# Seven block products for four up groups of a feed-forward layer, between plain groups

## The reference

```python
        h = rmsnorm(x, ffn_norm[l])
        u = causal_dwconv(h @ w_up[l], conv_w[l], conv_b[l])
        a, b = jnp.split(u, 2, axis=-1)
        x = x + (jax.nn.silu(a) * b) @ w_down[l]
```

## Time and profile before

| | us |
|---|---|
| median of three runs (2976.94 to 2977.67) | 2977.29 |
| span of the profiled execution, first to last instruction | 2976.6 |
| PE busy in it | 2947.6 |
| DVE, ACT, POOL busy | 1557.9, 1353.2, 1296.7 |
| layer 1: up groups 3 to 10 of the second block, from, to | 1652.47, 1826.68 |
| layer 2: the same, from | 2668.30 |

### The profile page before, as it was taken

How to read it: one execution, slowest core, us unless ns; L and a number is a source line. 1 busy time by engine, 2 the same in 40 slices (tenths; PEclk the granted TensorE clock), 3 DMA queues, 4 the chain that set the end, 5 groups by cost and what they waited for, 6 DMA issues and landing times.

```text
span 2976.6 us, 41216 instructions
## 1 busy us (share of the span) xinstructions
PE 2947.6 (99%) x15790; PEld 2434.6 (82%) x15790; DVE 1557.9 (52%) x2363; ACT 1353.2 (45%) x2286; POOL 1296.7 (44%) x926
## 2 busy tenths in 40 slices
PE   8999999999999999999999999999999999999998
PEld 7778887799988877788888888888787888888887
DVE  7974351497823978772116433178777511273312
ACT  6443344455533446663235443244566532354432
POOL 5335574410154543134555454554332354554443
PEclk9999999999999999999999999999999999999999
DMA  5334343233233523223333333244231233333332
GB/s 162 87 113 143 93 125 99 75 114 112 82 99 82 150 71 90 54 75 99 98 98 92 100 96 97 84 115 138 68 93 47 76 99 96 97 95 95 98 98 71
DMA packets 215041, 288.21 MB, mean 97 GB/s; under 512 B 42698, under 2 KB 122626, under 8 KB 213186
## 3 DMA queue, kind: packets, MB, share of 16 engines
q1 hardware_dynamic: 212354, 280.41, 32.4%
q0 software_dynamic: 880, 2.99, 0.3%
q10 hardware_dynamic: 1616, 2.23, 0.2%
HBM read 270.33 MB, written 4.72 MB: 92 GB/s over the span
## 4 chain that ended last, share of the span: by engine, by line
PE 91%; DVE 5%; ACT 2%; POOL 1%; issue 1%; DMA 0%; SPq 0%; ACTq 0%; DVEq 0%
PE half L872 76%; PE half L1202 2%; PE half L1205 2%; PE half L1204 2%; PE half L1341 2%; PE half L1355 2%; PE half L1319 1%; POOL wL L3438 1%; PE half L1324 1%; DVE arena L2416 1%; PE half L1417 0%; PE half L1127 0%; PE half L1144 0%; DVE rms L2407 0%; PE half L1042 0%
## 5 line engine op out<-in xcount | busy, mean ns | idle before, releaser
L3438 POOL TENSOR_TENSOR wL<-slot,wH 128x512 fp32r<-128x512 f32 (+1 forms) x904 | 1271.2, 1414 | 1650.7 <-ACT wH L1538 1649.6
L1538 ACT ACTIVATE wH<-slot 128x512 fp32r<-128x512 f32 (+1 forms) x904 | 558.1, 624 | 1067.0 <-PE half L872 1063.4
L872 PE MATMUL half<-nH,wH 128*128 128x512 f32 x2048 | 809.2, 395 | 4.3 <-ACT arena L1551 2.3
L872 PE MATMUL half<-nH,wL 128*128 128x512 f32 x2048 | 798.2, 390 | 0.0
L872 PE MATMUL half<-nL,wH 128*128 128x512 f32 x2048 | 797.7, 389 | 0.0
L872 PE MATMUL half<-arena_split,wH 128*128 128x512 f32 (+1 forms) x2432 | 735.8, 385 | 1.1 <-POOL wL L3438 0.6
L872 PEld LDWEIGHTS half<-arena_split,wH 128*128 128x128 f32 x2432 | 451.1, 188 | 93.7 <-POOL wL L3438 2.8
L872 PE MATMUL half<-arena_split,wL 128*128 128x512 f32 (+1 forms) x1216 | 466.4, 384 | 0.0
L872 PEld LDWEIGHTS half<-nH,wH 128*128 128x128 f32 x2048 | 384.4, 188 | 99.9 <-issue 19.8
L872 PEld LDWEIGHTS half<-nH,wL 128*128 128x128 f32 x2048 | 384.4, 188 | 82.0
L872 PEld LDWEIGHTS half<-nL,wH 128*128 128x128 f32 x2048 | 384.7, 188 | 78.0 <-issue 1.4
(11 more groups left out here) (406 smaller groups left out, 3606.8 us busy)
## 6 DMA issues: line engine op xcount, KB each, us to landing
slot<-in_w_in SPq DMA_DIRECT2D x344, 256.0 KB, 2.7
slot<-in_w_up SPq DMA_DIRECT2D x400, 128.0 KB, 2.2
slot<-in_w_down SPq DMA_DIRECT2D x132, 256.0 KB, 2.6
slot<-in_w_branch SPq DMA_DIRECT2D x64, 256.0 KB, 2.6
slot<-in_w_out SPq DMA_DIRECT2D x48, 256.0 KB, 2.7
arena<-arena SPq DMA_DIRECT2D x40, 256.0 KB, 4.4
slot<-in_w_gate SPq DMA_DIRECT2D x48, 128.0 KB, 2.3
arena<-in_w_gate SPq DMA_DIRECT2D x40, 128.0 KB, 2.3
```

What stands on the lines that cost most here:

```text
L872: mm = pe.matmul(dst, lhsT, rhs, start=(k == 0 and m == 0), stop=(k == last and m == 2))
L1538: act.activation(wH[:, p, 0:cols], slot[:, s, 0:cols], ACT.Copy).then_inc(weights_high, 1)
L3438: pool.tensor_tensor(wL[:, p, 0:cols], slot[:, s, 0:cols], plainly(wH[:, p, 0:cols]), ALU.subtract)\
```

## The change

In both layers of the second block, groups 3, 5, 7 and 9 become product groups; groups 0, 1, 2, 4, 6, 8, 10 stay plain. Tokens, sums and buffers follow the first block's scheme, with these differences:

- P1's result stays in bank 2 and P6 and P7 add to it there. ACT copies it on the way: P1 to bank 0, where P2 adds to it ("begun in PSUM"), and the running sum after P6 and after P7 to bank 3, P5's result to SBUF. DVE adds P5 to the copy of P6's sum, in bank 1, where P3 adds to it, and to the copy of P7's, in bank 3. So PSUM ends with the four blocks, and the taps read them there.
- The convolution is made in two halves (`conv_first` for `a`, `conv_second` for `b`), `a` in place in `ff_raw`, `b` in `second_kept` for one group at a time.
- The splitting of the whole product for the down projection (`whole_high`, `whole_rest`) is no longer made group by group, but after group 9.
- P4's token sum needs room: it lies on the tables of constants, which SP loads again in layer 1 after group 10, 2304 columns instead of 1024 in the branches' stage.
- Quads of the second block lie in `arena` (one set), each loaded in four pieces as soon as the last group's quad is read.

```diff
+LAYER_PRODUCTS = (3, 5, 7, 9)
-         [(f"up{g}", 8, 2) for g in range(NG)] + [("dn0", 22, 1), ("dn1", 22, 1)]]
+         [(f"up{g}", 7, 0) if g in LAYER_PRODUCTS else (f"up{g}", 8, 2) for g in range(NG)] + [("dn0", 22, 1), ("dn1", 22, 1)]]
...
-                for g in range(2):
-                    load(f"bdn{g}", lin(I["w_down_2"], l * FF, 512 * g), l)
+                load("bdn0", lin(I["w_down_2"], l * FF, 0), l, units=range(12))
+                if l + 1 < LAYERS:
+                    done(sp, f"bup{NG - 1}", l)
+                    sp.dma_start(tables, I["consts"][:, 2 * P:N_CONSTS - H]).then_inc(S["moved"], 16)
+                load("bdn0", lin(I["w_down_2"], l * FF, 0), l, units=range(12, NF))
+                load("bdn1", lin(I["w_down_2"], l * FF, 512), l)
...
+            def layer_products(g, l):
+
+                name, norm = f"bup{g}", "bss_ff"
+                o = fill(name, l)
+                product(name, "P1", o, l, fresh=True)
+                tokens_summed(norm, 0, l)
+                product(name, "P5", o, l, fresh=True)
+                tokens_summed(norm, 1, l)
+                kept_until(pe, "b", g, "P1", l)
+                product(name, "P6", o, l)
+                product(name, "P2", o, l)
+                tokens_summed(norm, 2, l)
+                kept_until(pe, "b", g, "U2", l)
+                product(name, "P7", o, l)
+                pe.wait_ge(S["fifth_added"], 2 * (l * len(LAYER_PRODUCTS) + LAYER_PRODUCTS.index(g)) + 1)
+                product(name, "P3", o, l)
+                tokens_summed(norm, 3, l)
+                kept_until(pe, "b", g, "U3", l)
+                product(name, "P4", o, l)
...
+                def other_products(g):
+
+                    name, i = f"bup{g}", l * len(LAYER_PRODUCTS) + LAYER_PRODUCTS.index(g)
+                    summed_until(act, "b", g, "S2", l)
+                    product_high(name, "P6", l)
+                    conv_first(g - 1)
+                    quad_seen(name, "A12", l)
+                    product_high(name, "P2", l)
+                    copy_bank(name, "P1", "P1", 0)
+                    conv_second(g - 1)
+                    summed_until(act, "b", g, "S3", l)
+                    product_high(name, "P7", l)
+                    keep(name, "P5", "P5", l)
+                    summed_until(act, "b", g, "S4", l)
+                    product_high(name, "P3", l)
+                    copy_bank(name, "U2", "P6", 3)
+                    conv_silu(g - 1)
+                    quad_seen(name, "A22", l)
+                    product_high(name, "P4", l)
+                    act.wait_ge(S["fifth_added"], 2 * i + 1)
+                    copy_bank(name, "U3", "P7", 3)
+                    ahead(f"bup{g + 1}", l)
+                    conv_first(g)
...
+                    product_rest(name, "P1", l)
+                    product_rest(name, "P5", l)
+                    sum_s4(name, l)
+                    product_rest(name, "P6", l)
+                    taps(g - 1, 0)
+                    product_rest(name, "P2", l)
+                    product_rest(name, "P7", l)
+                    taps(g - 1, 1)
+                    add_fifth(name, "U2", 1)
+                    product_rest(name, "P3", l)
+                    multiply(g - 1)
+                    product_rest(name, "P4", l)
+                    add_fifth(name, "U3", 3)
```

More of the change, by code:

```diff
@@ L94, with quads_in_slots, product_buffer @@
 QUAD_SEEN = {"A11": 1, "A21": 2, "A22": 2, "A12": 4}
+def quads_in_slots(stage, g):
+    return stage == "a" and g % 2 == 1
+def product_buffer(stage, g, nth):
+    return ((len(PRODUCTS) * (g - 2) if stage == "a" else 0) + nth + 2) % 3
 class Ring:
@@ new lines, in conv_silu, with copy_bank @@
+                def conv_silu(g):
+                    act.wait_ge(S["taps_added"], 2 * (l * NG + g) + 1)
+                    pair = ff_raw[:, 2 * g:2 * g + 2, :]
+                    act.activation(pair, pair, ACT.Silu).then_inc(S["silu"], 1)
+                def copy_bank(name, what, product, to):
+                    product_done(act, name, product, l)
+                    o, at = ps[jobs.half[name]], BANK["b"][product] * T
+                    act.activation(o[:, to * T:to * T + T], o[:, at:at + T], ACT.Copy).then_inc(S["products_kept"], 1)
@@ new lines, in _ @@
+                conv_first(0)
+                conv_second(0)
+                ahead("bup2", l)
+                conv_silu(0)
+                for n in range(4):
+                    token_sum_high("bss_ff", n, l)
+                conv_first(1)
+                round_units("bup2", l, 0, [4], 512)
+                conv_second(1)
+                round_units("bup2", l, 0, [5], 512)
+                conv_silu(1)
+                round_units("bup2", l, 0, [6, 7], 512)
+                for g in LAYER_PRODUCTS:
+                    first_products(g)
+                    other_products(g)
+                    conv_second(g)
+                    others(f"bup{g + 1}", l)
+                    conv_silu(g)
@@ L2367, in _ @@
+                for g in range(4):
+                    whole_high(g, before)
+                ahead("bdn0", l)
+                for g in range(4, NG - 1):
+                    whole_high(g, before)
+                conv_first(NG - 1)
+                round_units("bdn0", l, 0, [4], 512)
+                conv_second(NG - 1)
+                round_units("bdn0", l, 0, [5, 6], 512)
+                conv_silu(NG - 1)
+                whole_high(NG - 1, before)
                 if l + 1 < LAYERS:
@@ L2952, in product_rest @@
             def product_rest(name, what, l=0):
-                g = int(name[3:])
                 dve.wait_ge(weights_high, ring.at(ring.before, name, PRODUCTS.index(what), l, 0) + 1)
-                if g == FIRST_PRODUCTS and what == "P1":
+                if what == "P1" and (name[0] == "b" or name == f"aup{FIRST_PRODUCTS}"):
                     splits_until(dve, name, what, l)
-                high, low = product_weights(g, what)
-                rest(low, product_whole(g, what), high).then_inc(weights_split, 1)
@@ L2961, in whole_rest @@
-            def whole_rest(g):
-                dve.wait_ge(S["ff_high"], g + 1)
+                high, low = product_weights(name, what)
+                rest(low, product_whole(name, what), high).then_inc(weights_split, 1)
+            def whole_rest(g, before=0):
+                dve.wait_ge(S["ff_high"], before + g + 1)
                 rest(ff_rests[:, 2 * g:2 * g + 2, :], ff_raw[:, 2 * g:2 * g + 2, :], ff_high[:, 2 * g:2 * g + 2, :]).then_inc(S["ff_split"], 1)
@@ new lines, in _ @@
+                taps(0, 0)
+                taps(0, 1)
+                token_sum("bss_ff", 0, l)
+                token_sum("bss_ff", 1, l)
+                multiply(0)
+                token_sum("bss_ff", 2, l)
+                token_sum("bss_ff", 3, l)
+                for n in range(4):
+                    token_sum_rest("bss_ff", n, l)
+                sum_s1("bup3", l)
+                taps(1, 0)
+                taps(1, 1)
+                sum_s2("bup3", l)
+                sum_s3("bup3", l)
@@ L3401, in _ @@
+                taps(NG - 2, 0)
+                taps(NG - 2, 1)
+                multiply(NG - 2)
+                for g in range(4):
+                    whole_rest(g, before)
+                taps(NG - 1, 0)
+                taps(NG - 1, 1)
+                for g in range(4, 7):
+                    whole_rest(g, before)
+                multiply(NG - 1)
+                for g in range(7, NG):
+                    whole_rest(g, before)
                 if l + 1 < LAYERS:
@@ L3497, in _ @@
                 rests("bwo1", l)
-                for name in [f"bup{g}" for g in range(NG)] + ["bdn0", "bdn1"]:
-                    rests(name, l)
+                for g in range(NG):
+                    if g in LAYER_PRODUCTS:
+                        product_split(pool, f"bup{g}", "P4", l)
+                    else:
+                        rests(f"bup{g}", l)
+                rests("bdn0", l)
+                rests("bdn1", l)
 _SHAPES = {
```

272 lines of the change are left out of this document (157 added, 115 removed).

## The result

The changed kernel takes 2986.99 us (median; 2986.28 to 2987.56), the one before 2977.34 (2976.61 to 2978.39) in the same session: ratio 1.003, 95% interval 1.002 to 1.0041, 9.65 us slower. Forecast were 2978.1 us, with a range up to 2985 and 0.20 for slower. The profiled execution took 2986.8 us for a span of 2985.0.

A forecast was written before the change was run, and what follows sets the result against it. TensorE, busy 99% of 2976.6 us, was taken as the bound. Saving -12.6, head 2 x 4.0 and tail 2 x 2.7 made +0.8 us: 2978.1 us with the carried difference, range 2969 to 2985 (8 in 10).

The forecast's parts named there:

- 0.20 for slower: Chance of over +6 us, given to ACT's PSUM copy making product groups wait; 2983 us if in each group.
- The saving: Second block's eight product groups: each saves 1.58 us of matmuls, 12.6 us in all if PE never waits.
- no wait in the middle: Inside product groups: a question of order, not load; margins 1.0 to 3.0 us, so no loss taken.
- I take 4.0 a layer: Up group 2, head of the stage: PE waits for late-rounded units, so group 3 starts 4.0 us late per layer.
- both places: Up group 2: PE waits at unit 4 (1 to 2 us) and unit 6 (2 to 3 us).
- the releaser: Up group 2: POOL, handing over units 4 and 6, was to end PE's waits there.
- The walk's high end: Head, DVE and POOL in each other's way: unit 6 at 1651.3 to 1651.6, P1 4.3 to 4.5 us late.
- The tail: Start of the down projection: PE waits for late-rounded unit 7, 2.1 to 3.0 us, taken as 2.7 a layer.
- P1's rest: Start of group 3: not the limit; DVE comes to it at about 1655.7 to 1656.8, PE there at 1656.5.
- what lies around the span: Whole run: the median is 0.7 us above the profiled span of 2976.6, a difference carried over to the forecast.
- The copy rival: Product groups: PE waits before P6 for ACT's copy of P1, 0.65 us in each of 8; 2983 us, 0.20.

The follow-up runs named there:

- e3_dve: Changed kernel with only VectorE's queue reordered around group 3's start: two token rests moved later, rests of P1 and P5 moved earlier; 2981.03 us.
- e5_order: e4_all with VectorE making the rests of P6, P2, P7, P3, P4 ahead of group 2's taps, and some ScalarE work ahead of Silu(2); 2966.77 us.
- e1_act: Changed kernel with only ScalarE's queue reordered in up group 2: roundings of units 4 to 7 placed between token-sum high parts, ahead of Silu(1); 2993.91 us.
- e4_all: Changed kernel with the edits of e1_act, e2_tail and e3_dve together; 2979.12 us.
- e2_tail: Changed kernel with only ScalarE's queue reordered at the down projection's start: units 7 and 8 rounded earlier, unit 7 ahead of Silu(10); 2980.19 us.
- e8_code: e5_order with 60 waits on a long-set semaphore added at the head of PE's queue; 2965.84 us.
- 80 and 100 waits: Two runs of the kernel before, with 80 or 100 waits on a long-set semaphore at the head of PE's queue; 2978.84 and 2981.09 us.

## Why the prediction was wrong

- **The saving.** Right: 12.9 us (forecast 12.6), no wait in the middle, copy PSUM to PSUM 0.58 us, addition into PSUM 0.70, slivers 0.21, each as taken.
- **The failed step: "I take 4.0 a layer" for the head.** The mechanism, both places and the releaser were as forecast. The term measured 7.7 and 6.8. Two parts of it were missed. The smaller: without the clock group 3 is late by 5.0 us in each layer, where 4.0 were taken and 4.5 was the bound. The walk's high end, with DVE and POOL in each other's way, was the right one (unit 6 handed over at 1651.7, forecast 1651.3 to 1651.6): three DVE operations, the first token sum, the last token rest and S1, took 2.3 us each beside POOL, 1.1 more than alone, where 0.5 to 1 had been allowed, and DVE's taps of group 0 were done 0.8 us sooner than forecast (1631.1), which hid most of that. The larger: the sum had no term for PE's clock behind a wait, 2.7 and 1.8 us. That a wait costs only its own length was an assumption of the whole working. The Trainium skill (TensorE: Matmul & The Clock Gate, Part 1) says that the array falls to half its clock when PE has been idle and regains it by working; the 0.50 and the 0.43 us a matmul agree, and I had not weighed it. By removal the cause is shown: with the wait before unit 6 gone (e3_dve, e5_order) the clock stays at 1.00 in the head; with a new wait elsewhere (e1_act, e4_all) it falls there.
- **The tail.** Forecast 2.7, measured 2.75; e2_tail gave it back.
- **A step that was missing.** 1.35 us in the next layer's attention: a code transfer of PE fell among the partner copies. That the 576 more PE instructions of the first layer moved it there is inferred; what is shown is that instructions added at the head of PE's queue move it out (e8_code) and in (80 and 100 waits). Nothing in the working looked past the changed stage. The Trainium skill (Runtime: NRT & Kernel Launch, "Instruction fetch mechanics") has code come in 16 KiB blocks of 256 instructions and calls the cost of crossing from one to the next "mostly hidden"; the size agrees with the rows (16 KB, 130 transfers for 32732 matmuls and weight loads), and at the index dots the cost was not hidden.
- **P1's rest.** "Not the limit" was true only with the head late; e1_act shows it as the next wait.
- **Sum.** Head +6.5, attention +1.35, tail +0.1, middle -0.3: 7.6 of the 8.9 us by which the forecast was missed. Most of the rest, 1.1 us, comes from the line on "what lies around the span". The 0.7 us there are a median less the span of another execution. In every later run, of either kernel, a run's own time is 1.8 to 1.9 us above its own span, so a span of 2976.6 belongs to an execution of about 2978.4 us, 1.1 above the median of 2977.29, and the spans' difference of 8.4 us understates the medians' 9.65.
- **The rivals.** The copy rival did not happen: no product group waits. The time came out slower by another way, so the 0.20 for slower had been given for a cause that is not the one found. No rival had a head that costs more than its high end, nor a clock that falls.

## What to carry over

In this kernel a new wait of PE of 2.6 us or more cost its length and, in twelve of fourteen cases, 1.6 to 2.7 us more at half clock behind it; price it so, and look for it at both ends of a changed stage, where the neighbours' work stands in the same queues. Moving one engine's work earlier helps only if the engine behind it has the time: write out the due time of each operand and order the fullest queue by it, as e5_order does; 2967 us were in this change all along. Where PE's instruction count changes, look at the handovers behind it that wait for a DMA, even a layer further on.

## What the hardware showed that I had not expected

- The clock and the length of PE's wait, all traces, the first 20 us left out: after 1.1 to 1.7 us (eighteen waits) matmuls stayed at the full rate; after 2.6 us they fell to half the rate in four of six; after 3.3, 4.0 and 6.8 us in all eight, for 3 to 6 us, 1.6 to 2.7 us lost. The same wait at the same place fell out either way (tail: clock kept in the changed kernel, lost in e1_act and e3_dve).
- At the index dots, one 16 KB code transfer that begins 2.6 or 6.2 us behind the first of four 256 KB copies goes with a last copy 1.0 to 1.7 us late (6.04 to 6.71 us in all ten cases, 4.97 to 4.99 in the sixteen without one, both layers and all runs). In the other groups of copies such a start cost now nothing, now 0.6 us and more.
- POOL and DVE: a 128x1024 DVE operation with two SBUF inputs takes up to 2.3 us beside POOL's subtraction and 1.2 alone, so work that is moved earlier on ACT can make DVE slower by way of POOL (e1_act: 5.69 against 3.49 us).
